# Loading half of the first up and half of the first down matrix ahead of the second half of the output weights

## Time and profile before

| what | value |
|---|---|
| time, median of three executions | 1319.38 us (1319.28, 1319.38, 1321.90) |
| span of the profiled execution, first to last instruction | 1321.2 us |
| the profiled execution's own time | not listed apart; of the three times only 1321.90 us is longer than its span, and would leave 0.7 us around it |
| PE busy | 1250.6 us, 95% of the span |
| VectorE, ScalarE, GpSimd busy | 616.3, 202.1, 140.3 us |
| moved by DMA | 459.71 MB, 348 GB/s over the span |
| mean granted TensorE clock | 0.983 of full speed |

### The profile page before, as it was taken

How to read it: one execution, slowest core, us unless ns; L and a number is a source line. 1 busy time by engine, 2 the same in 40 slices (tenths; PEclk the granted TensorE clock), 3 DMA queues, 4 the chain that set the end, 5 groups by cost and what they waited for, 6 DMA issues and landing times.

```text
span 1321.2 us, 41309 instructions
## 1 busy us (share of the span) xinstructions
PE 1250.6 (95%) x16750; PEld 725.4 (55%) x16751; DVE 616.3 (47%) x1156; ACT 202.1 (15%) x380; POOL 140.3 (11%) x466
## 2 busy tenths in 40 slices
PE   9999999999999979699999999999999799999994
PEld 6777676476646545345555555555555455555552
DVE  0269995473236333234434443444344334434445
ACT  1111112343002101011111111111111111111111
POOL 1930000000001001001100110011000001100110
PEclk9999999999999989899999999999999999999997
DMA  9333334652898999999999999999999999999994
GB/s 307 112 111 122 127 127 149 165 172 87 322 415 341 428 429 430 434 428 430 430 437 429 429 432 434 426 431 436 430 428 422 430 431 428 430 431 437 431 430 178
DMA packets 61011, 459.71 MB, mean 348 GB/s; under 512 B 17324, under 2 KB 21148, under 8 KB 44057
## 3 DMA queue, kind: packets, MB, share of 16 engines
q1 hardware_dynamic: 60696, 459.03, 84.3%
q10 hardware_dynamic: 289, 0.33, 0.1%
HBM read 455.14 MB, written 4.73 MB: 348 GB/s over the span
## 4 chain that ended last, share of the span: by engine, by line
PE 87%; DMA 9%; issue 2%; DVE 1%; ACT 1%; SPq 0%; ACTq 0%; another core or an unknown queue 0%; DVEq 0%
PE PS L1392 28%; PE PS L1470 15%; PE PS L1107 13%; DMA SB<-in_w_down_dram 8%; PE PS L1380 6%; PE PS L1409 5%; PE PS L1282 3%; PE PS L1215 3%; PE PS L1170 2%; PE PS L1292 2%; PE PS L1411 2%; PE PS L1126 1%; PE PS L1136 1%; PE PS L1459 1%; PE PS L1399 1%
## 5 line engine op out<-in xcount | busy, mean ns | idle before, releaser
L1392 PE MATMUL PS<-SB 128*32 128x256 f32 x7424 | 431.1, 385 | 40.0 <-DMA SB<-in_w_up_dram 19.8
L1392 PEld LDWEIGHTS PS<-SB 128*32 128x32 f32 x7424 | 238.4, 111 | 217.6 <-issue 73.5
L1470 PE MATMUL PS<-SB 128*32 128x256 f32 x3712 | 213.9, 382 | 4.3 <-DMA SB<-in_w_down_dram 4.3
L996 DVE SCALAR_TENSOR_TENSOR SB<-PS,SB 128x1024 f32<-128x1024 f32 x176 | 193.6, 1100 | 7.2 <-PE PS L1409 2.9
L1008 DVE TENSOR_SCALAR PS<-PS 128x256 f32<-128x256 f32 x58 | 25.1, 432 | 326.8 <-PE PS L1399 326.8
L1107 PE MATMUL PS<-SB 128*128 128x320 f32 x640 | 172.8, 433 | 1.3 <-ACT SB L588 1.3
L1470 PEld LDWEIGHTS PS<-SB 128*32 128x32 f32 x3712 | 116.7, 110 | 83.8 <-DVE SB L1023 10.8
L1107 PEld LDWEIGHTS PS<-SB 128*128 128x128 f32 x640 | 121.4, 190 | 51.9 <-issue 1.5
L747 DVE SCALAR_TENSOR_TENSOR SB<-SB 128x350 f32<-128x350 f32 x240 | 118.5, 604 | 0.0
L686 ACT COPY SB<-PS 128x256 f32<-128x256 f32 x58 | 21.6, 372 | 609.4 <-PE PS L1470 609.4
L1380 PE MATMUL PS<-SB 128*32 128x256 f32 (+1 forms) x1416 | 96.6, 386 | 0.0
(11 more groups left out here) (245 smaller groups left out, 893.2 us busy)
## 6 DMA issues: line engine op xcount, KB each, us to landing
SB<-in_w_gate_dram SPq DMA_DIRECT2D x64, 2048.0 KB, 16.4
SB<-in_w_up_dram SPq DMA_DIRECT2D x30, 4096.0 KB, 22.7
SB<-in_w_down_dram SPq DMA_DIRECT2D x30, 4096.0 KB, 25.2
SB<-in_w_in_dram SPq DMA_DIRECT2D x13, 2048.0 KB, 8.1
SB<-in_w_up_dram SPq DMA_DIRECT2D x4, 2048.0 KB, 19.5
SB<-in_w_down_dram SPq DMA_DIRECT2D x4, 2048.0 KB, 16.4
SB<-in_w_pw_dram SPq DMA_DIRECT2D x2, 2048.0 KB, 8.3
SB<-in_w_att_o_dram SPq DMA_DIRECT2D x2, 2048.0 KB, 7.8
```

The lines of the kernel that those rows point to most:

```text
L996: dve.scalar_tensor_tensor(y, ps, gcol[:, tt:tt + 1], y, ALU.mult, ALU.add).then_inc(sem("yadd"), 1)
L1392: ins = pe.matmul(PS[32 * q:32 * q + 32, bank, 0:256], xg[:, c, :], buf[:, c, 256 * q:256 * q + 256], start=(c == 0), stop=False)
L1470: ins = pe.matmul(PS[32 * n:32 * n + 32, 2, 256:512], hT[:, ck, :], WD[par][:, ck, 256 * n:256 * n + 256], start=(ck == 0), stop=(ck == KC ...
```

## The change

1. `ga` and `ua` (with `zc` in its place) swap places in `wbuf[4]`: `ga` now lies at words 0 to 2559, `ua`/`zc` at 2560 to 5119. The second half of `wbuf[4]` then holds only `zc` and `gb`, which are dead once the last convolution product has been multiplied by its gate (`pw_evac` at 8).
2. The second half of `WU[0]` is loaded in step 1 of the list above, directly behind the first half, and no longer in step 4.
3. The second half of `WD[0]` is loaded between the two halves of `w_out`, after a wait for `pw_evac` at 8, and no longer in step 5. The first half stays in step 5.

The number of instructions on the compute engines and the bytes moved are the same.

```diff
-        ua = view(4 * WB, KC, T)
+        ga = view(4 * WB, KC, T)
+        ua = view(4 * WB + 2560, KC, T)
         zc = ua
-        ga = view(4 * WB + 2560, KC, T)
         gb = view(4 * WB + 5120, KC, T)
...
             sp.wait_ge(sem("p_mm"), PAIRS)
             load_halves(sp, WG[0], wg_v[0], "wg0")
-            load_half(sp, WU[0], wu_v[0], "wu0", 0)
+            load_halves(sp, WU[0], wu_v[0], "wu0")
             sp.wait_ge(sem("o_mm"), PAIRS)
...
-            for s in range(2):
-                group(s, w_out_v[:, :, s, :], "ao_mm", 4 * (s + 1))
+            group(0, w_out_v[:, :, 0, :], "ao_mm", 4)
+            sp.wait_ge(sem("pw_evac"), PAIRS)
+            load_half(sp, WD[0], wd_v[0], "wd0", 1)
+            group(1, w_out_v[:, :, 1, :], "ao_mm", 8)
             sp.wait_ge(sem("k_out"), 16 * 40)
-            load_half(sp, WU[0], wu_v[0], "wu0", 1)
             load_half(sp, WU[1], wu_v[1], "wu1", 1)
             sp.wait_ge(sem("mix_ready"), KC)
-            load_halves(sp, WD[0], wd_v[0], "wd0")
+            load_half(sp, WD[0], wd_v[0], "wd0", 0)
             load_half(sp, WU[1], wu_v[1], "wu1", 0)
```

## The result

The changed kernel takes 1326.40 us (median of five, 1326.36 to 1327.73) against 1319.38 us (median of five, 1319.08 to 1321.90): 7.0 us between the medians. The ratio of the two, taken over all executions, is 1.0048 (95% interval 1.0037 to 1.0058), which is 6.3 us (4.9 to 7.7). The profiled execution of the changed kernel took 1326.88 us at a span of 1325.2, so 1.7 us lie around a span.

What follows compares the result with a forecast made beforehand. The expert stream's start and rate were taken to bound the kernel up to 1063.8 us, then PE. Wait 3.35 plus clock 1.7 minus 0 gave +5.05 us, 1324.4 us; own range 1322.6 to 1325.6, wide range 1318.8 to 1327.6.

Steps and rivals of the forecast that it cites:

- The bound and the missing gain: Expert stream's start and rate bound the end to 1063.8 us, then PE; early loads gain 0 us, delays go through.
- The step that makes the loss: Early WU[0] half delays the first w_out half to 362.8 us; PE waits 3.35 us at its first w_out product.
- the price of a half in the full queue: Delay of the first w_out half by one more 2 MB half ahead of it in the queue: 4.9 us.
- The clock: After PE's idle time at the first output tile, its products run slower at a lower clock: 1.7 us.
- The half of `WD[0]`: Loaded between the w_out halves: cost 0, the second w_out half landing in time, hidden by 14 us of L1292.
- rival C: SP held at the early WD[0] half, second w_out half late, PE waits again at L1302: 1327.2 us; chance 0.08.
- The sum: Whole kernel: 3.35 + 1.7 - 0 = +5.05 us, median 1324.4 us, 0.38% slower.
- the forecast's own range: Kernel time from the low and high ends of wait and clock loss: 1322.6 to 1325.6 us.
- The signs: PE's w_out wait, issue near 351 us, clock 0.5, no L1302 wait, first gate load near 421, longer DMA idle.
- B: Small wait at the first output tile: laggard DMA engine catches up, clock holds; +1.5 us, 1320.9 us; chance 0.23.
- D: Queue's idle time from 356 to 359.5 us is used, expert stream starts 3.3 us earlier: 1316.1 us; chance 0.07.
- E: First expert block escapes its low clock and the stream takes up the rest: within 0.2%, 1319.4 us; chance 0.06.

Runs made afterwards that it cites:

- e2_down_only: The changed kernel with the second half of WU[0] loaded late as before; swap and early WD[0] half stay: 1321.8 us, ratio 1.0005.
- e3_up_behind: The changed kernel with the second half of WU[0] moved behind the first half of w_out: 1320.29 us, ratio 0.9999.
- e5_before_fill: The kernel before with six added products ahead of PE's first output tile, a pure delay of PE with loads on time: 1324.12 us, ratio 1.0030.
- e1_up_only: The kernel before with only the second half of WU[0] loaded directly behind the first: 1326.29 us, ratio 1.0046.
- e6_quarter: The kernel before with 1 MB of the second half of WU[0] loaded early, not 2 MB: 1322.34 us, ratio 1.0012.

## Why the prediction was right

**The bound and the missing gain.** Right. The early bytes are worth nothing (`e2_down_only`, `e3_up_behind`), since the stream starts with the tables. That a delay goes through to the end is shown as well: `e5_before_fill` passes on 4.0 us.

**The step that makes the loss.** Right in place and mechanism (`e1_up_only` has it alone, `e3_up_behind` takes it away), somewhat small in size. The wait was put at 3.35 us more than the kernel before; the changed kernel shows 5.15 - 1.16 = 4.0 us, `e1_up_only` 4.71 - 1.16 = 3.55. The 4.0 us lie above the 3.7 us that were the upper end. The term that was mis-sized is the price of a half in the full queue, 4.9 us. Counted from the first gate load, the first half of `w_out` landed 5.0 us later in `e1_up_only`, as priced, but 5.4 us later in the changed kernel. SP issued it 4.65 us later (it was held 21.07 us at L361 where it was 18.18, and longer at the issue before), and it took 12.42 us to land where it took 11.7. The two kernels differ in the `WD[0]` half right behind it; that this half took the 0.4 us is not shown.

**The clock.** Sized at 1.7 us from three falls of 1.35 to 2.5; measured 2.4, near the top end. The three rows could not place it better: the longest idle time among them, 7.12 us, had the smallest loss, 1.35. What sets the loss is how long PE works at half clock, here 4.8 us, and nothing in the rows before told that.

**The half of `WD[0]`.** Right: free, and hidden by L1292. The second half of `w_out` went out at 357.15 us and landed 15.3 us later, at 372.5, near the 372.6 forecast and 6.2 us before L1303 wanted it. Without PE's own delay there is no margin: in `e3_up_behind` it landed when it was wanted. SP was held 5.52 us at this issue in the changed kernel, but let go before 357.15, so rival C did not come.

**The sum.** +5.05 against +7.0 between the medians: 4.0 + 2.4 are explained, 0.6 are left, which is less than executions of one kernel differ by. The direction and the mechanism were right, and both terms came out too small. So 1326.40 us lies above the forecast's own range (1322.6 to 1325.6) and is covered only by the wide one, which ends at 1327.6. One statement on the profiled execution was wrong: a span has 1.7 us around it, not 0.7, so by estimate the profiled execution of the kernel before took 1321.2 + 1.7 = 1322.9 us, longer than any of its three times. The forecast did not depend on it, since the sum was put on the median.

**The signs.** Most were there: a wait for `in_w_out_dram`, the issue near 351 us (349.71), a clock of 0.50, no wait at L1303. Two were off: the first gate load came at 419.85 us and not near 421, and the idle stretch of DMA before it was shorter, not longer. The queue was down to a share of 0.08 for the 2.6 us before it, where it had been at 0.03 for 4.2 us, and the last of the twelve halves (issued at 408.8, 10.7 us to landing) landed only 0.3 us before the gate load, where it had been 2.0 us. Both come from the first expert block, which ran at full clock in this profile. So the statement that all twelve halves are there in time held, but with less room than the rows of before showed.

**Rivals.** B (1.5 us, the clock holds) fell: 4.0 us and a clock at half. D (faster) fell with `e3_up_behind`. E (nothing comes of it) named a real effect: at full clock the first expert block's 64 products took 3.66 us in the changed kernel where they took 5.34. But it belongs to the profiled execution, not to the kernels' difference: in `e1_up_only`, with the same delay, they took 5.35 us.

## What to carry to other kernels

An idle queue is worth filling only if something later waits for the bytes; look first at what the next load behind the idle time waits for. A prefetch put into a full queue delays the loads that are issued behind it, here by 5.0 to 5.4 us for 2 MB, and what exceeds such a load's slack (1.5 us here) is paid. So put the load with the nearest deadline first: the same 2 MB behind it showed no cost. Where PE has to wait anyway, a few products into an unused bank can keep its clock up; here they gave back 2.4 us of 6.4.

## What the runs showed that was not expected

The hold of SP at the router bias's load (L361 before) grew with what stood ahead: 18.18 us with three halves in front, 18.88 in `e6_quarter` (three and a half), 21.07 and 21.21 with four. A small issue behind a row of loads (here one of 16 KB) is where SP is stopped, and the first half of `w_out`, whose slot was free, could not go out. And the first expert block does not gain all that its clock gives: at full clock PE then waits 0.54 us for GpSimd, whose work for it starts only at 419.51 us (what it waited for until then, the profile doesn't show). The stream gains more: its gate loads go out 2.15 us after the first expert product (419.85 - 417.70), where it was 3.84 us.

```profile
417.70 3.66 PE L1393 MATMUL PS<-SB 128*32 128x256 f32 x64 [1.33 <-issue]
421.89 0.29 PE L1400 MATMUL PS<-SB 96*32 96x256 bf16 x4 [0.54 <-POOL SB L539]
...
419.51 0.41 POOL L524 TENSOR_TENSOR SB<-SB 128x96 f32<-128x96 f32 x1 [6.28 <-issue]
```
